# The second per-layer projection in front of the state space layer, its result through device memory

## The reference, cut to what matters

```python
x = x + rmsnorm(m, g[3])                                  # m: attention (layer 0) or s5_glu (layer 1)
x = x + 0.5 * rmsnorm(swiglu(rmsnorm(x, g[4]), ...), g[5])
gate = sigmoid(rmsnorm(x, g[6]) @ ple_w_gate[i])          # 1024 x 1024
x = x + rmsnorm(gate * (p[i] @ ple_w_proj[i]), g[7])      # p[i]: 256 x 256, ple_w_proj[i]: 256 x 1024
```

## Time and profile before

| what | value |
|---|---|
| median of 3 runs | 1632.83 us (1632.15 to 1633.04) |
| the profiled execution's own time | 1631.77 us |
| its span (first to last instruction) | 1629.9 us |
| TensorE busy | 1604.9 us, 98% |
| VectorE / ScalarE / GpSimd busy | 1143.1 / 931.1 / 170.1 us |
| granted TensorE clock, mean | 0.998 of full |

### The profile page before, as it was taken

One profiled execution on the slowest core, in us unless ns is written; L12 is line 12 of the kernel. 1 busy time (PEld: TensorE's weight loads), 2 busy tenths in 40 slices (PEclk: granted clock), 3 DMA queues, 4 the chain that ended last, 5 costly groups with the idle time before them and its releaser, 6 DMA issues.

```text
span 1629.9 us, 22903 instructions
## 1 busy us (share of the span) xinstructions
PE 1604.9 (98%) x8774; PEld 1349.7 (83%) x8774; DVE 1143.1 (70%) x1621; ACT 931.1 (57%) x1559; POOL 170.1 (10%) x240
## 2 busy tenths in 40 slices
PE   9999999999999999999999999999999999999997
PEld 7888799788888888878778888788889989788886
DVE  5666667789887766979776666756667776666665
ACT  6555566655567686552465556655555554655555
POOL 0000001128401112900000000000000000000000
PEclk9999999999999999999999999999999999999999
DMA  7877554567765665651666765577655434577662
GB/s 259 269 264 230 178 169 142 169 228 224 229 217 193 220 220 185 210 188 53 204 205 223 229 224 190 197 251 237 222 179 186 151 109 135 177 234 227 225 216 94
DMA packets 127053, 324.30 MB, mean 199 GB/s; under 512 B 14600, under 2 KB 48864, under 8 KB 126944
## 3 DMA queue, kind: packets, MB, share of 16 engines
q1 hardware_dynamic: 126496, 322.21, 60.7%
q0 software_dynamic: 160, 0.52, 0.1%
q10 hardware_dynamic: 288, 0.11, 0.0%
HBM read 307.54 MB, written 15.24 MB: 198 GB/s over the span
## 4 chain that ended last, share of the span: by engine, by line
PE 89%; DVE 5%; ACT 3%; issue 2%; POOL 0%; POOLq 0%; DVEq 0%; ACTq 0%
PE PS L2202 86%; PE PS L2347 1%; PE PS L2205 1%; DVE wlo L1377 1%; DVE wlo L1383 1%; ACT whi L791 1%; DVE SC L1725 0%; ACT SC L1010 0%; ACT wk L831 0%; PE PS L2641 0%; ACT whi L795 0%; DVE SC L1975 0%; ACT SC L1098 0%; ACT wk L858 0%; PE PS L2426 0%
## 5 line engine op out<-in xcount | busy, mean ns | idle before, releaser
L1383 DVE SCALAR_TENSOR_TENSOR wlo<-raw,ct,whi 128x512 fp32r<-128x512 f32 (+1 forms) x552 | 428.6, 821 | 197.3 <-ACT whi L795 197.1
L2202 PE MATMUL PS<-whi,xhi 128*128 128x512 f32 (+1 forms) x1312 | 500.1, 390 | 4.8 <-DVE wlo L1377 2.1
L2202 PE MATMUL PS<-wlo,xhi 128*128 128x512 f32 (+1 forms) x1312 | 494.9, 387 | 0.0
L795 ACT ACTIVATE whi<-raw,ct 128x512 fp32r<-128x512 f32 (+1 forms) x552 | 377.8, 734 | 199.4 <-PE PS L2202 183.7
L1377 DVE TENSOR_TENSOR wlo<-raw,whi 128x1024 fp32r<-128x1024 f32 x240 | 296.8, 1242 | 198.3 <-ACT whi L791 197.3
L2202 PE MATMUL PS<-whi,xlo 128*128 128x512 f32 (+1 forms) x1312 | 405.0, 387 | 0.0
L791 ACT ACTIVATE whi<-raw 128x1024 fp32r<-128x1024 f32 x240 | 252.8, 1057 | 241.8 <-PE PS L2202 234.4
L2202 PEld LDWEIGHTS PS<-whi,xhi 128*128 128x128 f32 x1312 | 245.8, 188 | 60.1 <-DVE wlo L1377 4.2
L2202 PEld LDWEIGHTS PS<-whi,xlo 128*128 128x128 f32 x1312 | 246.4, 188 | 50.6
L2202 PEld LDWEIGHTS PS<-wlo,xhi 128*128 128x128 f32 x1312 | 246.5, 188 | 48.9
L2202 PE MATMUL PS<-whi,hhi 128*128 128x512 f32 x544 | 173.4, 392 | 0.5 <-DVE hlo L1577 0.4
(11 more groups left out here) (286 smaller groups left out, 1492.7 us busy)
## 6 DMA issues: line engine op xcount, KB each, us to landing
raw<-in_w SPq DMA_DIRECT2D x528, 512.0 KB, 4.7
blocks<-wk SPq DMA_DIRECT2D x54, 256.0 KB, 3.3
wk<-blocks SPq DMA_DIRECT2D x216, 64.0 KB, 2.4
gr<-in_rows SPq DMA_DIRECT2D x14, 512.0 KB, 3.9
SC<-scratch SPq DMA_DIRECT2D x5, 512.0 KB, 5.4
X<-in_x SPq DMA_DIRECT2D x2, 512.0 KB, 5.2
SC<-scratch SPq DMA_DIRECT2D x4, 256.0 KB, 5.4
xn<-in_sc SPq DMA_DIRECT2D x2, 512.0 KB, 7.9
```

Source lines behind the costliest of these rows:

```text
L795: e = a.activation(hi[:, f], src[:, f], ACT.Copy, scale=ct[:, c:c + 1])
L1383: e = v.scalar_tensor_tensor(lo[:, f], src[:, f], ct[:, c:c + 1], hi[:, f].bitcast(f32), MUL, SUB)
L2202: return pe.matmul(o, l, r, start=start, stop=stop)
```

## The change

The projection of layer 1 becomes units 240 and 241 and stands ahead of the state space layer, whose gated unit moves to 242. Its input `pT[1]` is loaded and split (`ple_start(1)`) in `ffn(2)` instead of `ffn(3)`. TensorE runs its 24 products right behind `ffn(2)`, in the place of the 25 idle ones, into banks 4 to 7. ScalarE copies one half of the tokens into `wk`, SyncE stores it to a new tensor in device memory (`spl`, "projected"), ScalarE waits for the store (`l_prs`), copies the second half, SyncE stores that, and only then ScalarE writes `decay` into `wk`. Before `start(4)` the result is loaded into `prj`. Permuting uses banks 0 to 3 and waits for each half row of `xn`. The six idle products behind the permutation are gone. `ple(1)` has no projection left: its order is transposes of h = 0, gate for h = 0, transposes of h = 1, gate for h = 1. The semaphore `l_snk` is merged into `l_b1`.

```diff
-FFN_AT = (0, 98, 174, 256, 332, 452)
-ATTN_AT, PLE_AT, GLU_AT, MIX_AT = 66, (164, 322, 518), 240, 398
+FFN_AT = (0, 98, 174, 258, 332, 452)
+ATTN_AT, GLU_AT, MIX_AT = 66, 242, 398
+PROJ_AT, GATE_AT = (164, 240, 518), (166, 324, 520)
+PLE_START = {1: 0, 2: 1, 5: 2}
...
# SyncE
             weights(LAST["ffn2"] - 1)
+            for h in range(2):
+                q.wait_ge(s_prj, n_prj(1, h))
+                sp.dma_start(spl[h], wk[:, :]).then_inc(l_prs, 16)
             q.wait_ge(s_ys, 2)
...
-            ple_in(1)
+            q.wait_ge(s_X, n_x(6, 1))
+            q.wait_ge(l_prs, 32)
+            for h in range(2):
+                sp.dma_start(prj[:, h, :], spl[h]).then_inc(l_prs, 16)
...
# ScalarE
             def s5():
+                q.wait_ge(s_sq, n_sq(PLACED, 1))
+                projected(1, 0)
+                use(GLU_AT - 2)
+                q.wait_ge(l_prs, 16)
+                projected(1, 1)
+                ahead.done = LAST["proj1"]
                 use(GLU_AT)
+                q.wait_ge(l_prs, 32)
...
# VectorE, place_u and s5
-                b = (4, 6)[h]
+                b = (0, 2)[h]
...
                     if m == 0:
-                        use(GLU_AT)
+                        use(GLU_AT - 2)
+                        ahead.done = LAST["proj1"]
...
+                        if m == 0 and z in (0, 8):
+                            use(GLU_AT - 1 + z // 8)
...
# TensorE
-                    q.wait_ge(s_xn, n_two(k, h))
                     q.wait_ge(s_perm, 1)
-                    b = (4, 6)[h]
+                    b = (0, 2)[h]
                     for m in range(2):
+                        q.wait_ge(s_xn, n_two(k, h, m))
...
+                if layer == 1:
+                    transposed(k, 0)
+                    linear("gate1", x_acts, 4, head=2, tail=2, by_half=k, between=lambda: transposed(k, 1))
+                    return
...
             def s5():
-                for n in (1, 2):
-                    q.wait_ge(s_u, n)
-                    fill_in(0, GLU_AT, 3)
                 q.wait_ge(s_cst, 16)
                 for m in range(2):
                     q.wait_ge(s_u, m + 3)
+                    if m:
+                        q.wait_ge(s_prj, 4)
...
             ffn(2)
             bg.drain()
+            q.wait_ge(s_plo, 2)
+            run([(PROJ_AT[1] + i, *p_acts[i], i == 0, i == 1) for i in range(2)], 4, True)
             settle(5)
             s5()
```

More of the change, by code:

```diff
@@ L79 @@
 LAST.update(v0=ATTN_AT + 3, v2=ATTN_AT + 17, v3=ATTN_AT + 23, wo=ATTN_AT + 31, glu1=GLU_AT + 11, glu2=GLU_AT + 15, w_out=MIX_AT + 53)
-LAST.update({f"proj{i}": PLE_AT[i] + 1 for i in range(3)})
-LAST.update({f"gate{i}": PLE_AT[i] + 9 for i in range(3)})
+LAST.update({f"proj{i}": PROJ_AT[i] + 1 for i in range(3)})
+LAST.update({f"gate{i}": GATE_AT[i] + 7 for i in range(3)})
 QK_AT = [(4 if h < 6 else 6) + 2 * h for h in range(8)]
@@ L115, with n_prj @@
     for kt in range(8):
-        G_COLS[PLE_AT[layer] + 2 + kt] = (COL_G + 48 + 8 * layer + kt,)
+        G_COLS[GATE_AT[layer] + kt] = (COL_G + 48 + 8 * layer + kt,)
+def n_prj(layer, h):
+    return 2 * layer + h + 1
 def pair_bank(n):
@@ L203, in upto, with program @@
             yield self.n - 1
-def program(nc, w, rows, cols, pT, b1c, ssm_s, ssm_b, ssm_c, ssm_cc, oh, idn, eo, x, out, scr, blk):
+def program(nc, w, rows, cols, pT, b1c, ssm_s, ssm_b, ssm_c, ssm_cc, oh, idn, eo, x, out, scr, blk, spl):
     f32, f32r, i32 = mybir.dt.float32, mybir.dt.float32r, mybir.dt.int32
@@ L590, in ple_in @@
             def ple_in(layer):
-                q.wait_ge(s_X, n_x((2, 6, 10)[layer], 1))
+                if layer == 1:
+                    q.wait_ge(s_plo, 1)
+                else:
+                    q.wait_ge(s_X, n_x((2, 6, 10)[layer], 1))
                 sp.dma_start(pr_t, pT[layer]).then_inc(l_pr, 16)
@@ L615, in sync @@
                 sp.dma_start(d, ssm_b[i]).then_inc(l_bc, 16)
+            weights(up_at(1, 5))
+            ple_in(1)
             settle_rows(3)
@@ L948, in ffn @@
                     silu(j, 1)
-                    if j == 3 and n % 2:
-                        ple_start(n // 2)
+                    if j == 3 and n in PLE_START:
+                        ple_start(PLE_START[n])
                     if j:
@@ L973, in ple_start, with projected @@
                 a.activation(phi[:, 0:2, :], pr_t, ACT.Copy).then_inc(s_phi, 1)
+            def projected(layer, h):
+                if h:
+                    q.wait_ge(s_used, LAST[f"proj{layer}"] + 1)
+                else:
+                    q.wait_ge(s_y, LINEARS.index(f"proj{layer}") + 1)
+                a.activation(wk[:, :] if layer == 1 else prj[:, h, :], flat(4 + 2 * h), ACT.Copy).then_inc(s_prj, 1)
             def ple(layer):
                 k = (3, 7, 11)[layer]
[L978 to L985, removed]
                 def rest():
@@ L992, in ple @@
                 squares(k, 1)
[L993 to L998, removed]
+                if layer == 1:
+                    use(GATE_AT[1])
+                    evict_hi(k, 0)
+                    evict_hi(k, 1)
+                else:
+                    use(PROJ_AT[layer])
+                    evict_hi(k, 0)
+                    projected(layer, 0)
+                    evict_hi(k, 1)
+                    projected(layer, 1)
+                    ahead.done = PROJ_AT[layer] + 1
                 linear(f"gate{layer}", 8, head=2, tail=2, finish=rest)
@@ L1423, in gated @@
                 q.wait_ge(s_gate, n_part(k, h, i))
-                if k != 6:
-                    q.wait_ge(s_prj, 2 * (4, 8, 12).index(k) + h + 1)
+                if k == 8:
+                    q.wait_ge(l_prs, 64)
+                elif k != 6:
+                    q.wait_ge(s_prj, n_prj((4, 8, 12).index(k), h))
                 else:
@@ L1621, in ple @@
                 k = (3, 7, 11)[layer]
-                v0 = LAST[f"proj{layer}"] - 1
                 gate_or_low(k, 0)
@@ L1628, in ple @@
                 add_x(k, 1)
-                use(v0)
+                use(GATE_AT[1] if layer == 1 else PROJ_AT[layer])
                 evict_lo(k, 0)
                 evict_lo(k, 1)
-                ahead.done = v0 + 1
+                if layer != 1:
+                    ahead.done = PROJ_AT[layer] + 1
                 linear(f"gate{layer}", 8, head=2, tail=2)
@@ L2503, in ple @@
                                 e.then_inc(s_y if c else s_half, 1)
-                q.wait_ge(s_prj, 2 * layer + 1)
+                q.wait_ge(s_prj, n_prj(layer, 0))
                 linear(f"gate{layer}", x_acts, 4, head=2, tail=2, by_half=k,
-                       between=lambda: q.wait_ge(s_prj, 2 * layer + 2))
+                       between=lambda: q.wait_ge(s_prj, n_prj(layer, 1)))
             def bias_tiles(k):
```

30 lines of the change are left out of this document (18 added, 12 removed).

## The result

Over 20 executions of each kernel the changed one has a median of 1633.67 us (1631.98 to 1645.93), the kernel before 1632.33 us (1631.08 to 1633.22). The ratio is 1.0025, with a 95% interval from 1.0013 to 1.0037. The median lies 0.4 us from the predicted 1633.3, in part by luck: the forecast stood on a median of 3 executions, 0.5 us above that of the 20. The rise of the median is 1.34 us, where 0.45 was forecast. The ratio is near that of the means (1636.30 / 1632.34 = 1.0024), and it tells the two kernels apart, because the changed kernel's times form two groups. Fifteen lie between 1631.98 and 1635.50 us (middle 1633.21) at a mean TensorE clock of 0.997 or 0.998; five lie between 1643.79 and 1645.93 at 0.989 or 0.990. Of the kernel before none is in the upper group. The means differ by 3.96 us.

A forecast was written before the change was run, and what follows sets the result against it. TensorE was busy for 98% of the span, but VectorE was taken to set the pace at the changed places. +0.5 us at the state space layer and -0.05 at ple(1) gave +0.45: 1633.3 us, range 1631.8 to 1635.8.

The forecast's parts named there:

- Steps 1 and 2: Before the state space layer: 24 products replace 25 idle (gain 0.22 us); half-row permuting, no idle products behind, inputs 0.65 us earlier.
- Step 2: Permuting by half rows without idle products behind it: state inputs start 0.65 us earlier, VectorE free for splits at 734.8.
- the rival of 0.04: At ple(1): TensorE's gaps drop the clock to 1.2 GHz, costing 5.4 us over the gate's first 24 products, 1638.7; chance 0.04.
- Step 3: State space layer: two more splits between VectorE's steps, partly absorbed by waits, start the sum 0.5 us later; about +0.5 us.
- Step 4: Stores of the projection's result: landing in some 4 us, free up to 5.5, so hidden; no cost.
- Step 5: ple_start(1) moved into ffn(2), and loading the 1 MB result: hidden, no cost; uncovered it would cost 0.6 us.
- Step 6: ple(1) without the projection: 5.4 us of products turn into 5.3 us of waits; gate for h = 1 gains 0.05 us.
- waits three times, some 5 us: Profile sign of being right: at ple(1) TensorE waits three times, some 5 us in all.
- The rival "the clock falls at ple(1)": At ple(1), TensorE nearly idle from 999 to 1002.5: clock halves to 1.2 GHz, 5.4 us slower, 1638.7; chance 0.04.
- the row of 2.01 us busy: Evidence against a clock fall: a trace stretch with TensorE busy 2.01 of 4 us kept the full 2.4 GHz.
- The sum +0.45: Whole kernel: +0.5 us before the state space layer, nothing for stores and loads, -0.05 at ple(1); +0.45 us in all.

The follow-up runs named there:

- a_s5_idle: Changed kernel with six idle products put back behind the permutation, with plain operands (0.43 us a pass): lower median 1637.52 us, kernel before on that chip 1632.58.
- a_mix_idle: Changed kernel plus 14 idle products of 256 columns in a VectorE wait in the mixers: lower median 1632.19 us, kernel before 1632.62; 4 of 12 executions above 1640.
- b_late: Kernel before with 9 idle products instead of 6 behind the permutation, starting everything after it 0.65 us later: median 1634.12 us, kernel before on that chip 1633.02.

## Why the prediction failed, step by step

- **Steps 1 and 2, order of events: right.** VectorE is free for its splits at 734.25 + 0.60 = 734.85 (forecast 734.8). The inputs start 0.45 us earlier, forecast 0.65, since the second turning came 0.11 us later than I put it (732.97 + 0.60 = 733.57) and the inputs 0.83 us behind it instead of 0.75.
- **Step 2, "no idle products behind it": this failed.** I asked what those six products delayed, and not what they covered. The sum took them at nothing but a later start. Without them TensorE idles for 0.90 us between the permutation and matmuls of 64 columns, and in 21 of 100 executions the clock then lies at 1.2 GHz for 27.3 us, for 12 us of time. A loss of the clock I priced at `ple(1)` alone, as the rival of 0.04.
- **Step 3: right.** The sum starts 0.45 us later, forecast 0.5. It is the splits' 1.02 us less the 0.57 by which the sum would come earlier without them: 0.32 through the turning and 0.25 through the inputs, which stand behind no idle products.
- **Step 4: right.** The store took 2.6 us to land; I allowed 4 and up to 5.5. ScalarE waits 0.79 us twice, and VectorE never for `whi`.
- **Step 5: right.** The distance to the profile of before is 0.6 us at the first transposes and at the end of `ffn(2)`, and the delay is 0.45 us at the sum and at the last product of `ffn(3)` (998.60 + 0.60 against 998.75), so nothing was lost in `ffn(2)` or behind the scans.
- **Step 6: right.** Three waits at `ple(1)` (0.87, 1.16, 1.21 us) and a fourth of 1.07 for the second half, which step 6 had in its sum but "waits three times, some 5 us" did not count; together they are 4.31 us. The gate's start moved by 0.03 us, forecast 0.05.
- **The rival "the clock falls at ple(1)"** had the right mechanism at the wrong place. By the Trainium skill (TensorE: Matmul & The Clock Gate, "Part 4: PE-mode transpose") transposes don't count as busy, which pointed at this stretch; it showed 1.00 in both groups' profiles. Of the six profiles with this order in `ple(1)` and no cover, only that of a_s5_idle, which came there late, has a short dip (0.66 in the window 1008 to 1012, the row below). Against the rival I set the row of 2.01 us busy that kept the clock. That row was one execution's: it is the stretch in the mixers where the short dip comes in other executions.
- **The sum +0.45** holds in the trace: up to the gate for h = 1 the delay is 0.42 us (1008.78 + 0.60 against 1008.96). By whole times it is not shown: at a mean clock of 0.998 or 0.999 a_mix_idle's seven executions have a median of 1632.07 us and the 19 of the kernel before on that chip 1632.37. The lower group's 0.9 us is, as an estimate, this and the small dip: 0.87 of its executions are at 0.997, where 0.45 were of the kernel before in the later batches, at 1.3 us each, which is 0.55 us. That share was not in the forecast either; b_late shows that a delay of such a size brings it.

```profile
1008.00:1012.00 4.00, 3.25 (x8) 2.13 (x8) 4.00 (x6) 1.19 (x3) 0.00 (x0) 0.66 0.51 170
```

## What to carry to other kernels

An idle product has two prices: what it delays, and the clock that it holds. Before one is removed, look at what TensorE does on both sides of the gap that it leaves, and take more than one execution, since one profile at full clock is no proof that the clock is safe. When a projection leaves a place where the next work waits for an eviction, nothing is won until the order on the evicting engines changes with it: here, with the projection gone, the order was worth 1.9 to 3.0 us at the gate's start, and the move alone nothing (0.03 us).

## What I had not expected of the hardware

One program has two times 12 us apart with the same instructions and the same gap of 0.90 us, in the same minutes on the same chip; only the granted clock tells them apart (0.989 against 0.997). The interval at the half level was 27.3 us long in both profiles that caught it, although TensorE is busy for 4.00 of every 4 us from 740 to 764 us, and 3.4 us in each of the shorter dips. Being 0.65 us late made the share of executions at 0.997 (the short dip) go from 16 of 34 executions to 10 of 11. What decides within the changed kernel which execution falls is not shown.
